# Modulation vectors inside the layers: partial sums folded to 64 rows, both conditions summed in the two row halves of TensorE

## What is computed

```python
sc, scc = silu(c), silu(c_ctx)
for l in range(DEPTH):                                   # DEPTH = 2
    m  = (sc  @ w_mod[l] + b_mod[l]).reshape(bsz, N_MOD, 1, D_MODEL)   # N_MOD = 9, D_MODEL = 1024
    mc = (scc @ w_mod[l] + b_mod[l]).reshape(N_MOD, D_MODEL)
    h  = h  + 0.5 * m[:, 2] * swiglu(modulate(h,  m[:, 0], m[:, 1]), w_ff1_in[l], w_ff1_out[l])
    hc = hc + 0.5 * mc[2]   * swiglu(modulate(hc, mc[0],   mc[1]),   w_ff1_in[l], w_ff1_out[l])
    ...                                                  # mixer with m[3..5], second feed-forward with m[6..8]
```

## Time and profile before

| | us |
|---|---|
| median of the runs | 3370.18 (3364.86 to 3372.57) |
| the profiled execution | 3373.55 |
| its span, first to last instruction | 3371.8 |
| TensorE matmul busy | 3236.4 (96%) |
| VectorE busy | 1583.1 (47%) |
| ScalarE busy | 964.5 (29%) |
| mean granted TensorE clock | 0.977 of full speed |

### The profile page before, as it was taken

One profiled execution on the slowest core, in us unless ns is written; L12 is line 12 of the kernel. 1 busy time (PEld: TensorE's weight loads), 2 busy tenths in 40 slices (PEclk: granted clock), 3 DMA queues, 4 the chain that ended last, 5 costly groups with the idle time before them and its releaser, 6 DMA issues.

```text
span 3371.8 us, 44352 instructions
## 1 busy us (share of the span) xinstructions
PE 3236.4 (96%) x18259; PEld 2927.0 (87%) x18259; DVE 1583.1 (47%) x2328; ACT 964.5 (29%) x1453; POOL 266.5 (8%) x316
## 2 busy tenths in 40 slices
PE   5999999999999999899999999999999998999999
PEld 4999999987669894478999999999999976678887
DVE  6744536424552636636624354442225457743333
ACT  3211212346441321133212112321212345732222
POOL 1100000200001005620000001000000100000000
PEclk8999999999999999999999999999999999999999
DMA  5533424311004220014513242232224220023332
GB/s 185 174 100 100 125 65 139 117 44 52 7 1 126 63 65 4 1 38 121 160 57 94 75 125 88 82 94 60 65 63 142 65 63 14 2 81 94 100 94 94
DMA packets 381726, 272.91 MB, mean 81 GB/s; under 512 B 17410, under 2 KB 357625, under 8 KB 381433
## 3 DMA queue, kind: packets, MB, share of 16 engines
q1 hardware_dynamic: 356217, 182.50, 18.6%
q0 software_dynamic: 25344, 88.09, 8.4%
HBM read 262.16 MB, written 8.39 MB: 80 GB/s over the span
## 4 chain that ended last, share of the span: by engine, by line
PE 90%; ACT 4%; DVE 2%; issue 2%; POOL 1%; DMA 1%; SPq 0%; ACTq 0%; DVEq 0%
PE ps L458 75%; PE ps L671 2%; PE ps L1216 1%; PE ps L1111 1%; PE ps L1337 1%; PE ps L1191 1%; PE ps L1197 1%; PE ps L1207 1%; PE ps L1707 1%; ACT gpt L1369 1%; PE ps L1741 1%; PE ps L1014 1%; PE ps L1724 1%; PE ps L1708 1%; DMA u_sb<-in_ctx 1%
## 5 line engine op out<-in xcount | busy, mean ns | idle before, releaser
L458 PE MATMUL ps<-u_hi,w_hi 128*128 128x384 f32 (+2 forms) x2992 | 827.8, 346 | 18.6 <-DVE u_lo L599 13.6
L448 DVE TENSOR_TENSOR w_lo<-ring,w_hi 128x1024 fp32r<-128x1024 f32 (+3 forms) x357 | 415.6, 1165 | 870.0 <-ACT w_hi L433 676.0
L458 PE MATMUL ps<-u_hi,w_lo 128*128 128x384 f32 (+2 forms) x2992 | 821.7, 344 | 0.0
L458 PE MATMUL ps<-u_lo,w_hi 128*128 128x384 f32 (+2 forms) x2992 | 820.9, 344 | 0.0
L458 PEld LDWEIGHTS ps<-u_hi,w_hi 128*128 128x128 f32 x2992 | 541.4, 189 | 46.3 <-issue 22.4
L458 PEld LDWEIGHTS ps<-u_lo,w_hi 128*128 128x128 f32 x2992 | 542.0, 189 | 22.5 <-issue 1.7
L458 PEld LDWEIGHTS ps<-u_hi,w_lo 128*128 128x128 f32 x2992 | 541.3, 189 | 21.0
L433 ACT CAST w_hi<-ring 128x1024 fp32r<-128x1024 f32 (+3 forms) x229 | 221.6, 969 | 1039.0 <-PE ps L458 992.9
L458 PE MATMUL ps<-hid_hi,w_hi 128*128 128x384 f32 (+1 forms) x1232 | 344.6, 349 | 0.0
L458 PE MATMUL ps<-hid_lo,w_hi 128*128 128x384 f32 (+1 forms) x1232 | 343.3, 348 | 0.0
L458 PE MATMUL ps<-hid_hi,w_lo 128*128 128x384 f32 (+1 forms) x1232 | 342.0, 347 | 0.0
(11 more groups left out here) (261 smaller groups left out, 3298.1 us busy)
## 6 DMA issues: line engine op xcount, KB each, us to landing
ring<-in_w_ff_in SPq DMA_DIRECT2D x176, 512.0 KB, 3.8
m_in<-in_w_mod POOLq DMA_DIRECT2D x128, 512.0 KB, 4.0
ring<-in_w_ff_out SPq DMA_DIRECT2D x64, 512.0 KB, 3.6
ring<-in_w_in_e SPq DMA_DIRECT2D x26, 512.0 KB, 3.8
ring<-in_w_ff_out SPq DMA_DIRECT2D x32, 384.0 KB, 3.1
m_first<-in_w_mod POOLq DMA_DIRECT2D x16, 512.0 KB, 13.3
ring<-in_w_out_e SPq DMA_DIRECT2D x16, 512.0 KB, 3.7
ring<-in_w_in_o SPq DMA_DIRECT2D x12, 512.0 KB, 3.7
```

Of the source, the lines that this page charges most:

```text
L448: dve.tensor_tensor(w_lo[:, b:b + WIDE[n]], ring[:, s:s + WIDE[n]], w_hi[:, b:b + WIDE[n]], ALU.subtract).then_inc(w_split_lo, 1)
L458: mm = pe.matmul(ps_at(p, c0, c1) if halved else pair(p)[:, c0:c1], w, x[:, c0:c1], start=start and i == 0, stop=stop and i == 2)
```

## The change

For the ten jobs that `pe_out` runs (`HALVED`), VectorE adds the two halves of the partitions as soon as a job's last piece is added: `dve_fold` puts the sum of the first condition into rows 0 to 63 of its part of `m_sum` and that of the second condition into rows 64 to 127 of its part. It is called in `dve_mod_piece` behind the last `m_add` of a job, after a wait for that add. `pe_mod_halves` takes the place of `pe_mod` in `pe_out`: the same 16 products, but each over 64 rows, the first condition in the upper and the second in the lower row half, into two different PSUM banks (`HALF_BANKS`; slot 2 uses the banks of slot 0 again and waits until VectorE has read them). It waits for the new semaphore `m_fold`. `dve_mod` reads the two conditions from the two banks. The eight other jobs stay as they are.

```diff
@@ dve_mod_piece
             m_add(dve, m_in[:, D * (n % 2):D * (n % 2) + D], k, slot_)
+            if k == DB - 1 and x in HALVED:
+                dve.wait_ge(m_used, n + 1)
+                dve_fold(dve, x, slot_)
+
+        HALVED = [x for key in sorted(MODS) if key not in MODS_AT.values() for x in MODS[key]]
+
+        HALF_BANKS = ((4, 7), (5, 6), (4, 7))
+
+        def dve_fold(dve, x, slot_):
+
+            c, e = D * 2 * slot_, D * 2 * slot_ + D
+            n = HALVED.index(x) + 1
+            dve.tensor_tensor(m_sum[0:64, c:c + D], m_sum[0:64, c:c + D], m_sum[64:128, c:c + D], ALU.add)
+            dve.tensor_tensor(m_sum[64:128, e:e + D], m_sum[0:64, e:e + D], m_sum[64:128, e:e + D],
+                              ALU.add).then_inc(m_fold, 1)
+
+        def pe_mod_halves(pe, x, slot_):
+
+            pe.wait_ge(m_fold, HALVED.index(x) + 1)
+            top, low = HALF_BANKS[slot_]
+            if slot_ == 2:
+                pe.wait_ge(mod_raw, JOB[x] - 1)
+            for d in range(DB):
+                c0 = 16 * x[1] + 2 * d
+                c, e = D * 2 * slot_ + P * d, D * (2 * slot_ + 1) + P * d
+                pe.matmul(bank(top, c0, c0 + 1), m_sum[0:64, c:c + P], ones[0:64, 0:1], start=True, stop=True)
+                mm = pe.matmul(bank(low, c0, c0 + 1), m_sum[64:128, e:e + P], ones[64:128, 0:1],
+                               start=True, stop=True)
+            mm.then_inc(m_mm, 1)
@@ dve_mod
             g, q = x
+            other = x in HALVED
+            if other:
+                top, low = HALF_BANKS[slot_]
+                first = top - slot_
...
-                y = dve.scalar_tensor_tensor(out=m[:, q, :, s], in0=raw[:, :, s],
+                y = dve.scalar_tensor_tensor(out=m[:, q, :, s], in0=raw[:, :, s] if not other or not s else
+                                             bank(low, 16 * q, 16 * q + 16).rearrange(
+                                                 "p (d s) -> p d s", s=2)[:, :, 0],
@@ pe_out
                 if d < len(mods):
-                    pe_mod(pe, mods[d], d, mods_used(*src))
+                    pe_mod_halves(pe, mods[d], d)
```

More of the change, by code:

```diff
@@ L273, in build @@
         m_came = [sem(f"m_came{i}") for i in range(8)]
-        m_used, m_mm, mod_raw, mod_done = sem("m_used"), sem("m_mm"), sem("mod_raw"), sem("mod_done")
+        m_used, m_fold, m_mm, mod_raw, mod_done = sem("m_used"), sem("m_fold"), sem("m_mm"), sem("mod_raw"), sem("mod_done")
         n_sq, n_ss, n_ln, n_rs, n_t, n_u = (sem("n_" + s) for s in ("sq", "ss", "ln", "rs", "t", "u"))
```

## The result

The changed kernel takes 3355.82 us in the median (3353.17 to 3356.61), the kernel before in the same runs 3371.38 us (3364.86 to 3374.73): a ratio of 0.995, 95% interval 0.9939 to 0.9961. It is 15.6 us faster (13 to 21 us by that interval); forecast were 3359 us and a gain of 11 to 13.

The account below looks back on a forecast made before the run. TensorE matmuls bound the kernel (90% of the chain). Batches 21.3, clock 6.6, stalls 9.6 and their clock 4 make 41.5 us against 54.6: 13 off 3373.55, less half of 3.4 execution excess, gives 3359 us; range 3345 to past 3373.

Parts of the forecast that it names:

- The batch: TensorE, ten modulation batches behind output blocks: about 2.1 us each by half-height loads, 21 us against 36.3, 15 us less.
- the four items of switching: TensorE, per batch beside 1.76 us of loads: 0.10 and 0.09 us switching, 0.03 last column, 0.11 open load.
- The five terms: TensorE, one new batch: 0.10 + 1.76 + 0.03 + 0.09 + 0.11, about 2.1 us.
- rival 1: TensorE batches: the halves take turns, 3.8 us a batch, a fall behind all ten, 3387 us; chance 0.08.
- The clock: Blocks behind the ten batches: four in ten followed by a fall of 1.66 us, 6.6 us instead of 18.3.
- The folds: VectorE, two 64 x 1024 additions a job at 1.22 us each: 2.5 us a job, 25 us in all.
- The stalls: TensorE before output block 0 in (0,0) and (1,0): folds delay the weight split, idle 4.8 us each, 9.6 us.
- Their clock: TensorE behind the two stalls in (0,0) and (1,0): a half-speed stretch costing 2 us each, 4 us.
- Rival 2: Blocks behind the batches: the clock falls behind every one all the same, about 3369 us; chance 0.17.
- rival 3: Before output block 0: no stall, folds cheaper than their nearest row or a wait misread, about 3345 us; chance 0.08.
- Rival 4: VectorE folds cost twice the row, stalls of 12 us in both places, about 3374 us; chance 0.05.

Follow-up runs that it names:

- Experiment 3: Changed kernel, but both conditions' products use the upper 64 rows, so the halves can't run side by side: 3389.36 us, ratio 1.0036 to the kernel before.
- Experiment 6: Experiment 1 with each batch doing its first two blocks twice, so a stretch without streaming lasts 2.43 us: 3352.48 us, ratio 0.9943 to the kernel before.
- experiment 2: Changed kernel with its folds and two banks, but the batches' products at full height again (128 rows): 3384.35 us, ratio 1.0031 to the kernel before.
- Experiment 1: Changed kernel with the folds of a part's second and third job moved behind weight split, last product and low half: 3344.75 us, ratio 0.9909 to before.
- experiment 5: Experiment 1 with each half-height batch cut in two, the second piece in the middle of the next output block: 3340.16 us, ratio 0.991 to before.

## Why the prediction was right, point by point

The batch. Forecast 2.1 us each by 16 loads and the four items of switching read from the earlier trace rows; measured 2.10. Ten give 15 us, as forecast. (The five terms add up to 2.09; the forecast's sum carries ten of them as 21.3 us. And the other modulation jobs are eight, not seven.) Experiment 3 shows that the gain is the halves' running side by side, the contrary of rival 1: there a batch that takes turns has 3.77 us for a forecast of 3.8, and the kernel 3389 us for a forecast of 3387. L689's first pass (422.92) starts before L688's second (423.04), where rival 1 needed it to wait. The Trainium skill, in "TensorE: Matmul & The Clock Gate", Part 3, says that matmuls start and end strictly in program order. That fits these rows as long as whole products are meant, since each L688 starts before its L689 (422.91 and 422.92). For the two passes of an fp32 product it does not fit, if the program lists them product by product, as they ran in experiment 3; no row shows the program's own list.

The clock. Forecast four falls in ten behind batches, 6.6 us; three, at 1.60 us, 4.8 us. The term was right within its bounds, but its ground was too simple. I took 1.64 and 2.33 us as lengths up to which none and from which on every stretch is followed by a fall. Experiment 6 has six stretches of 2.43 us without one, experiment 2 one of 3.5 us, and in the changed kernel's trace one of 1.63 us at 1276 is followed by a fall 2.3 us behind its end, which in the trace of before was not. The trace of before already had such a case, which the prediction overlooks where it says that of eleven such stretches none was followed by a fall. The same line's stretch before 1366.87, as long as the one before 1290.64, is followed by a fall 2.1 us behind its end (PE in order of time; then a stretch with its granted clock, columns of rows 3):

```profile
1366.87 0.71 PE L1645 MATMUL ps<-bc 128*128 128x128 f32 x4 [1.47 <-DVE st L1632]
...
1368.96:1375.70 6.74, 5.92 (x14) 0.50 0.00 0
```

In both cases TensorE did little between the stretch and the fall (groups of four 128-column matmuls, with 0.35 and 0.18 us of idle time before two of them), so the stretch alone need not be the cause. Four in ten was a choice between two lengths of which neither is sharp; that three came is partly luck.

The folds. Forecast 1.22 us for each instruction and 2.5 for a job: L675 1.221 and L676 1.222 us on average; from 190.57 to 193.06 a job adds 2.6 us with what lies between. Half the partitions take the same time, as the earlier trace rows let expect. Starts of neighbouring instructions are 1.13 us apart where they overlap (186.93 to 188.06) and 1.23 to 1.26 at the folds. That agrees with the Trainium skill's rule in "VectorE: DVE Perf Modes", section "Two Vector instructions with no wait between them".

The stalls. Forecast 4.8 us in (0,0) and in (1,0); the table gives 5.23 and 5.19. Of the 0.4 us more, 0.3 are the folds (three of 2.6 us instead of 2.5), and the rest is the 0.15 us from the end of the split (203.93 + 1.22 = 205.15) to TensorE's start at 205.30, which the forecast's slack left out. The last add's DMA wait was swallowed as forecast. (0,1), (1,1) and (2,0) have none, as forecast. Their clock: forecast 2 us each; 11.90 - 10.42 = 1.5 and 11.67 - 10.42 = 1.3, so 2.7 instead of 4. Experiment 1, which takes only the place away, gains 12.7 us, each against its own kernel before (11 us between the medians), for a forecast 13.6 and a measured sum of 10.4 + 2.7 = 13.1; it also had one fall fewer behind its batches, 1.6 us, so the sum is some 2 us more than the runs give.

The sum. -15.3 (batches) - 13.5 (clock behind them) + 10.4 (stalls) + 2.7 (their clock) = -15.7 us by terms, -15.5 us by the table, -15.6 us in the medians. That the last agrees so closely is luck, since the interval reaches from 13 to 21 us and the two traces differ by 17.9. The forecast's -13.1 was low by 1.8 us at the clock, 1.3 at the stalls' clock and 0.3 at the batches, with 0.8 the other way at the stalls. Rival 2 (a fall behind each) and rival 3 (no stall) are out by the profile. Rival 3's time, 3345 us, is what experiment 1 takes, where the stalls are gone: 3344.75. Rival 4 (dear folds) is out by the folds' 1.22 us.

## What to carry to other kernels

A short piece of light TensorE work between dense blocks costs its own time and often a stretch of half clock behind it. Cut into pieces of 1.7 us and spread, the same instructions lost nothing more here, and that single edit was worth at least as much as the whole rework of the sums. It does not add up with it: on the half-height batches, of which few were followed by a fall, the cut paid as much for its second switch as it saved (experiment 5). Count the falls in the trace before cutting. Work that VectorE can spare in the sum still costs one for one where it stands ahead of the one result that TensorE needs next: list what queues behind a new instruction, find the latest place at which its own user is still served in time, and put it there. Two half-height products side by side take the time of one, with 0.3 us for going to halves and back.

## What the runs showed of the hardware

- One-column products in both row halves: a pair of loads every 0.11 us, where one full-height load takes 0.11 us; the same products in one half alone take turns (0.22 us a product), so the row count of a load has no part in its time.
- Going from full height to halves and back adds 0.27 us up to the next block's first matmul (3.77 against 3.50 us for 32 loads), and 0.32 us from block to block (10.75 with two pieces against 10.43 with one).
- Behind 2.43 us without streaming the clock fell four times in ten, behind 3.5 us it stayed once in twenty: neither length is safe or certain. Of forty pieces of 1.09 or 1.71 us between dense blocks none was followed by a fall. Among lighter work, at 1366.87 in the trace of before and at 1276 in the changed kernel's, stretches of 1.6 us were.
- A fall behind a batch cost 1.56 to 1.66 us where it was measured and the clock came back within the block; the longest low stretch, behind the batch at 1895 before, cost 2.8 us.
